# One root for two norms between two blocks, and the context normed during the last down projection

## The reference

```python
def rmsnorm(x, g):
    xf = x.astype(jnp.float32)
    y = xf * lax.rsqrt(jnp.mean(xf * xf, axis=-1, keepdims=True) + EPS)
    return (y * g.astype(jnp.float32)).astype(x.dtype)
...
        x = x + (jax.nn.silu(g) * u) @ w_down[i]
    return rmsnorm(x, final_g)
```

```python
def modulate(a, g, shift, scale):
    return rms_norm(a, g) * (1 + scale) + shift
...
        h_lat = modulate(x, norm_g[layer], sh_l, sc_l)
        h_ctx = modulate(ctx, norm_g[layer], sh_c, sc_c)
```

## Time and profile before

| | |
|---|---|
| median of 3 runs | 2828.7 us (2828.47 to 2835.98) |
| profiled execution | 2831.81 us, its span 2830.0 us |
| granted TensorE clock, mean | 0.963 |
| PE busy | 2604.9 us, 92% |
| PEld busy | 2114.6 us, 75% |
| DVE busy | 1117.6 us, 39% |
| ACT busy | 991.3 us, 35% |
| POOL busy | 975.6 us, 34% |

### The profile page before, as it was taken

How to read it: one execution, slowest core, us unless ns; L and a number is a source line. 1 busy time by engine, 2 the same in 40 slices (tenths; PEclk the granted TensorE clock), 3 DMA queues, 4 the chain that set the end, 5 groups by cost and what they waited for, 6 DMA issues and landing times.

```text
span 2830.0 us, 33844 instructions
## 1 busy us (share of the span) xinstructions
PE 2604.9 (92%) x13182; PEld 2114.6 (75%) x13182; DVE 1117.6 (39%) x2054; ACT 991.3 (35%) x1811; POOL 975.6 (34%) x515
## 2 busy tenths in 40 slices
PE   5999899999999989999869989999999998898888
PEld 4775688888676668888657878878877887786666
DVE  2136589520324559841151121430112242355564
ACT  3335344432434444442232232211222222344442
POOL 4322255754422135675432222322222222321121
PEclk9999899999999989999979999999999999899999
DMA  4111154222311125422211000111100021110000
GB/s 165 68 34 60 60 183 175 97 92 94 105 53 41 60 94 196 138 99 95 92 38 45 23 30 23 60 60 60 45 23 31 30 68 47 61 60 23 31 31 30
DMA packets 53869, 199.52 MB, mean 71 GB/s; under 512 B 5968, under 2 KB 5968, under 8 KB 52944
## 3 DMA queue, kind: packets, MB, share of 16 engines
q1 hardware_dynamic: 51696, 188.65, 19.5%
q10 hardware_dynamic: 2016, 8.71, 0.9%
HBM read 195.24 MB, written 2.10 MB: 70 GB/s over the span
## 4 chain that ended last, share of the span: by engine, by line
PE 85%; DVE 5%; ACT 3%; POOL 3%; issue 2%; DMA 1%; ACTq 0%; POOLq 0%; DVEq 0%
PE ps L507 54%; PE ps L527 12%; PE ps L557 7%; PE ps L832 5%; PE ps L704 3%; POOL wl L2182 1%; POOL norm_acc L2195 1%; PE ps L1026 1%; PE ps L719 1%; DVE norm_sq L1633 1%; ACT wh L1063 1%; PE ps L706 0%; POOL norm_sq L2277 0%; PE ps L839 0%; PE ps L1011 0%
## 5 line engine op out<-in xcount | busy, mean ns | idle before, releaser
L2182 POOL TENSOR_TENSOR wl<-wring,wh 128x1024 fp32r<-128x1024 f32 (+1 forms) x305 | 761.8, 2498 | 1418.5 <-ACT wh L1063 1408.1
L1063 ACT ACTIVATE wh<-wring 128x1024 fp32r<-128x1024 f32 (+1 forms) x305 | 317.0, 1042 | 771.4 <-PE ps L507 765.7
L507 PE MATMUL ps<-hh,wh 128*128 128x512 f32 x1224 | 481.7, 394 | 20.4 <-DVE hl L1645 16.0
L507 PE MATMUL ps<-hl,wh 128*128 128x512 f32 x1224 | 480.5, 393 | 0.0
L507 PE MATMUL ps<-hh,wl 128*128 128x512 f32 x1224 | 480.3, 392 | 0.0
L507 PEld LDWEIGHTS ps<-hh,wh 128*128 128x128 f32 x1224 | 232.1, 190 | 74.7 <-DVE hl L1645 15.7
L507 PEld LDWEIGHTS ps<-hh,wl 128*128 128x128 f32 x1224 | 231.6, 189 | 49.0
L507 PEld LDWEIGHTS ps<-hl,wh 128*128 128x128 f32 x1224 | 231.8, 189 | 47.3 <-issue 0.5
L557 PE MATMUL ps<-arena 128*128 128x64 f32 (+2 forms) x720 | 186.9, 396 | 14.4 <-ACT arena L1267 6.2
L1669 DVE CUSTOM_DVE_ANT_0 arena<-arena 128x1024 f32<-128x1024 f32 x96 | 185.8, 1935 | 9.0 <-DVE arena L1845 0.5
L557 PEld LDWEIGHTS ps<-arena 128*128 128x128 f32 x720 | 109.0, 197 | 85.3 <-issue 58.2
(11 more groups left out here) (263 smaller groups left out, 4941.4 us busy)
## 6 DMA issues: line engine op xcount, KB each, us to landing
wring<-wts SPq DMA_DIRECT2D x290, 512.0 KB, 3.5
arena<-wts SPq DMA_DIRECT2D x48, 512.0 KB, 4.3
wring<-wts SPq DMA_DIRECT2D x16, 384.0 KB, 2.9
xL<-xt SPq DMA_DIRECT2D x1, 2048.0 KB, 9.6
arena<-tab SPq DMA_DIRECT2D x1, 2048.0 KB, 16.8
arena<-cv ACTq DMA_DIRECT2D x2, 1024.0 KB, 5.5
arena<-tab ACTq DMA_DIRECT2D x1, 2048.0 KB, 9.0
out_t<-xL ACTq DMA_DIRECT2D x8, 256.0 KB, 2.0
```

Source lines behind the costliest of these rows:

```text
L507: mm = nc.tensor.matmul(o[0], a, b, start=start and k == first and j == 0, stop=stop and k == last and j == 2)
L1063: nc.scalar.activation(wh[:, sn % SPLIT_SLOTS, :kn * w], raw(u)[:, :kn * w], ACT.Copy).then_inc(act_done, tick("act", ("hi", u)))
L2182: G.tensor_tensor(wl[:, sn % SPLIT_SLOTS, :kn * w], raw(u)[:, :kn * w], wh[:, sn % SPLIT_SLOTS, :kn * w].bitcast(F32), ALU.subtract).then_inc(
```

## The change

- `mL` is no longer made from `fin`'s result. ScalarE squares each new `xL` tile twice during the down projection: once as it is (`fin`) and once scaled by `fgn[:, m]` (`mL`), the absolute final gain, made at the kernel's start by Square, Ln and Exp of eight columns. One root of the second sum, with `eps2` = EPS x EPS in place of EPS, scales `xL` straight to `hH` and `hLo`, with the gain `fgm` (final gain times modulation gain). `fin` gets its own scratch at `NF` and bank 6, and its root and scaling come after `mL`'s.
- The context is loaded into `xct`, over `hH`, after the last up projection, squared and added behind the split of `dn 0,1`, summed by TensorE after j = 0, its root made in j = 1, and its split pass done in j = 3, after the split of `dn 3,2` on ScalarE and before `xL` tile 6 on the vector engine. It is then loaded a second time, into `xC`.
- TensorE does the context's gate columns (now banks 4 and 5), `norm(("mL",0))`, the context's query columns, `norm(("fin",0))`, and then for each of the 8 tiles the latents' gate columns and both latent query tiles. `project_qk(0)` has only `("mqk",0,1)` left.
- The split of `("mqk",0,0)` moves between the last squares and additions.

The core of the diff:

```diff
-            norm(("fin", 0))
-            norm(("mC", 0))
-            norm(("mL", 0))
-            for m in range(KT):
-                pe.wait_ge(dve_done, at("dve", "hl", ("mC", 0), m))
+                    if l == DEPTH - 1 and j == 0:
+                        norm(("mC", 0))
...
-            def hm_ready(k):
+            (gate_unit,), query_units = views(("gate",)), views(("mqk", 0, 0))
+            gate_all, hc = slice(0, 100), (lambda k: hcH[:, k, :], lambda k: hcL[:, k, :])
+            for m in range(KT):
+                pe.wait_ge(dve_done, at("dve", "hl", ("mC", 0), m))
+            claim([4, 5], "dve", "glf")
+            product(ps[0:100, 4, 256:512], rows(gate_all, *hc), [gate_unit])
+            norm(("mL", 0))
+            for i in range(2):
+                claim([2 * i, 2 * i + 1], "act", "mqk", 0, i)
+            for u in query_units:
+                for i in range(2):
+                    product(ps[:, 2 * i, 256:512], rows(side(i), *hc), [u], start=u is query_units[0],
+                            stop=u is query_units[1])
+            norm(("fin", 0))
+            for k in range(KT):
                 pe.wait_ge(dve_done, at("dve", "hl", ("mL", 0), k))
-
-            claim([0, 1], "dve", "glf")
-            project(("gate",), both(0, 100, slice(0, 100), ("gate",)), hm_ready)
+                u, first, _, v = query_units[k // 4]
+                end = k == KT - 1
+                product(ps[0:100, 5, :], lat(gate_all), [(gate_unit[0], k, 1, [r[:, k:k + 1, :] for r in gate_unit[3]])],
+                        *([("gate",), ("used", gate_unit[0])] if end else []), start=k == 0, stop=end)
+                for i in range(2):
+                    product(ps[:, 2 * i + 1, :], lat(side(i)), [(u, k, 1, [r[:, k - first:k - first + 1, :] for r in v])],
+                            *([("mqk", 0, i)] if end else []), *([("used", u)] if i and k % 4 == 3 else []),
+                            start=k == 0, stop=end)
...
+            nc.scalar.activation(fgn[:, 0:8], col("fin", 0, 8), ACT.Square).then_inc(act_done, tick("act"))
+            act.wait_ge(act_done, now("act"))
+            nc.scalar.activation(fgn[:, 0:8], fgn[:, 0:8], ACT.Ln, bias=col("eps")).then_inc(act_done, tick("act"))
+            act.wait_ge(act_done, now("act"))
+            nc.scalar.activation(fgn[:, 0:8], fgn[:, 0:8], ACT.Exp, scale=0.5).then_inc(act_done, tick("act", ("fgn",)))
...
+                if last:
+                    act.wait_ge(pe_done, at("pe", "up", l, 2 * FT - 1))
+                    act.dma_start(xct.rearrange("p k t -> p (k t)"), ct).then_inc(ctx_loaded, 16)
+                    act.wait_ge(pool_done, at("pool", "gul", l, FT - 1))
+
+                def square_both(m):
+                    square(("mL", 0), m, ("xd", l), fgn[:, m:m + 1])
+                    square(("fin", 0), m, ("xd", l))
...
+                        if last and (j, c) == (0, 0):
+                            act.wait_ge(ctx_loaded, 16)
+                            for m in range(KT):
+                                square(("mC", 0), m)
+                        if last and (j, c) == (1, 0):
+                            root(("mC", 0))
+                        if last and (j, c) == (3, 1):
+                            high(("mC", 0), hcH, 1)
+                            act.wait_ge(pe_done, at("pe", "used", units_of[("dn", l, 3, 1)][-1]))
+                            act.dma_start(xC.rearrange("p k t -> p (k t)"), ct).then_inc(ctx_loaded, 16)
...
+            split(("mqk", 0, 0), first)
+            square_both(6)
+            square(("mL", 0), 7, ("xd", DEPTH - 1), fgn[:, 7:8])
+            split(("mqk", 0, 0), second)
+            square(("fin", 0), 7, ("xd", DEPTH - 1))
             root(("mL", 0))
             high(("mL", 0), hH, 0)
-            split(("mqk", 0, 0))
+            root(("fin", 0))
...
+                    if l == DEPTH - 1 and m == 6:
+                        dve.wait_ge(dve_done, now("dve"))
+                        V.tensor_tensor(fgn[:, 8:16], mscv[:, 0, 0, 0:8], col("fin", 0, 8), ALU.mult).then_inc(
+                            dve_done, tick("dve", ("fgm",)))
+                        dve.wait_ge(pe_done, at("pe", "used", units_of[("dn", l, 3, 0)][-1]))
+                        scaled_split(("mC", 0), lambda m: mscv[:, 0, 1, m:m + 1], hcH, hcL, 1)
...
+            scaled_split(("mL", 0), lambda m: fgn[:, 8 + m:9 + m], hH, hLo, 0)
             scaled(("fin", 0), lambda m: col("fin", m), xL)
-            scaled_split(("mC", 0), lambda m: mscv[:, 0, 1, m:m + 1], hcH, hcL, 1)
-            scaled_split(("mL", 0), lambda m: mscv[:, 0, 0, m:m + 1], hH, hLo, 0)
...
+                        if last and (j, c) == (0, 0):
+                            accumulate(("mC", 0))
...
+                    elif j < 3:
+                        for m in (2 * j, 2 * j + 1):
+                            accumulate(("mL", 0), m)
+                            accumulate(("fin", 0), m)
+            split(("mqk", 0, 0), slice(0, 1))
+            accumulate(("mL", 0), 6)
+            accumulate(("fin", 0), 6)
+            accumulate(("mL", 0), 7)
+            split(("mqk", 0, 0), slice(1, 2))
+            accumulate(("fin", 0), 7)
```

More of the change, by code:

```diff
@@ L132, in param_columns @@
     at, n = {}, 0
-    for name, width in [("eps", 1), ("ln1", 16), ("ln2", 16), ("fin", 8), ("ng", 16), ("qn", 4), ("kvn", 2),
+    for name, width in [("eps", 1), ("eps2", 1), ("ln1", 16), ("ln2", 16), ("fin", 8), ("ng", 16), ("qn", 4), ("kvn", 2),
                         ("dn", 2), ("fb", 2), ("conv", DEPTH * 4 * 2 * FT), ("lam", DEPTH * 256), ("adab", 48),
@@ L279, in program @@
         msc = place("msc", 32)[0]
+        fgn = place("fgn", 16)[0]
         arena, ar = place("arena", ARENA)
@@ L1309, in _ @@
                         load_exp_ln()
-                after = ("ln1", l + 1) if l + 1 < DEPTH else ("fin", 0)
+                last = l + 1 == DEPTH
+                if last:
[5 more added lines that the diff above has]
+                    square(("fin", 0), m, ("xd", l))
                 for j in range(4):
@@ L1314, in _ @@
                             split(("dn", l, j, c + 1) if c < 2 else ("dn", l, j + 1, 0))
[L1315 to L1330 removed]
+                        else:
+                            split(("gate",) if last else ("cq", l + 1))
+                        if last and (j, c) == (0, 0):
[8 more added lines that the diff above has]
+                            act.dma_start(xC.rearrange("p k t -> p (k t)"), ct).then_inc(ctx_loaded, 16)
+                    if not last:
+                        square(("ln1", l + 1), 2 * j, ("xd", l))
+                        square(("ln1", l + 1), 2 * j + 1, ("xd", l))
+                    elif j < 3:
+                        square_both(2 * j)
+                        square_both(2 * j + 1)
+            split(("mqk", 0, 0), first)
[3 more added lines that the diff above has]
+            square(("fin", 0), 7, ("xd", DEPTH - 1))
             root(("mL", 0))
             high(("mL", 0), hH, 0)
[L1333 removed]
+            root(("fin", 0))
             act.wait_ge(dve_done, at("dve", "glf"))
@@ L2263, in _ @@
                             split(("dn", l, j, c + 1) if c < 2 else ("dn", l, j + 1, 0))
-                        elif l + 1 < DEPTH:
-                            split(("cq", l + 1))
-                        else:
-                            split(("gate",))
-                    accumulate(after, 2 * j, 2 * j + 1)
-            accumulate(("mC", 0))
-            accumulate(("mL", 0))
-            split(("mqk", 0, 0))
+                        else:
+                            split(("gate",) if last else ("cq", l + 1))
+                        if last and (j, c) == (0, 0):
+                            accumulate(("mC", 0))
+                    if not last:
+                        accumulate(("ln1", l + 1), 2 * j, 2 * j + 1)
+                    elif j < 3:
+                        for m in (2 * j, 2 * j + 1):
[7 more added lines that the diff above has]
+            accumulate(("fin", 0), 7)
             def rows_norm(h):
@@ L2395, in layout @@
     put("eps", 0, np.full((P, 1), EPS, np.float32))
+    put("eps2", 0, np.full((P, 1), EPS * EPS, np.float32))
     put("idn", 0, np.eye(P, dtype=np.float32))
```

53 lines of the change are left out of this document (25 added, 28 removed).

## The result

The changed kernel takes 2803.68 us (median of 4 runs, 2797.8 to 2804.29) beside 2829.41 us for the kernel before on the same chip (2828.47 to 2835.98). The ratio is 0.9896, with a 95% interval of 0.9882 to 0.9910: 1.0% faster. The profiled execution took 2804.22 us with a span of 2802.2; the profiled one of before took 2831.8 with 2830.0. The forecast was 2800.6 us, with a range of 2795.5 to 2806.

A forecast was written before the change was run, and what follows sets the result against it. TensorE, busy 92% of the span, bounds the kernel; its standstills around the last down projection can be won. 28.75 us won less 0.7 at the start gives 28.05: 2828.7 to 2800.6 us, range 2795.5 to 2806.

The forecast's parts named there:

- Norm of `mC` between two chunks: Last down projection: the context's sum on TensorE between two chunks costs 0.5 us, between nothing and 1.12.
- No stall of the down projection: Context squares and doubled additions cost TensorE nothing there, with 3.0 us and 3.5 us of cover.
- rival B: Down projection stalls because squares or additions use up the cover; 2802 to 2806 us, chance 0.10.
- Pass of the context, 1.5 us added: Context's scaling pass during the down projection: 6.7 us plus 1.5 beside a GpSimd split, last high part at 1399.2.
- Rival A: Vector engine and GpSimd exclude each other only on scans, so added terms go: 2.7 us less, 2797.9; chance 0.12.
- C: Context not ready early; its pass and gate split slip behind the down projection: 2811 us, chance 0.04.
- Sum of `mL`, 1408.8: Behind the down projection: TensorE starts the norm of `mL` at 1408.8, after GpSimd's splits and additions.
- 1.25 us for the addition beside the pass: Latents' pass: GpSimd's last `fin` addition beside it adds 1.25 us by exclusion; term between 0 and 1.27.
- Eight steps at full clock: Latents' gate and query columns: 72 matmuls take 16.8 us without waiting, to 1433.1.
- rival D: TensorE stays at clock 0.50 through the eight steps after resting before the norm: +14.7 us, 2815; chance 0.04.
- What is late next: `fin` root and scaling, gate reads, soft-plus, then splits of `("mqk",0,1)`: TensorE idles 10.5 us, 1433.1 to 1443.6.
- The second half, 1443.6 to 1463.15: Query/key projection: second unit at 1446.6, 84 matmuls in 15.5 us, 1.05 for low clock; end at 1463.15.

The follow-up runs named there:

- e5: Changed kernel with two roots again: only `fin` squared in the down projection, `mL` squared from its scaled result; 2812.42 us, ratio 0.9944.
- e6: Changed kernel with splits and evacuations ahead of the soft-plus, plus four more moves, among them `fin` scaled behind the gate reads; 2796.98 us, ratio 0.9896.
- e1: Changed kernel with ScalarE's splits of `("mqk",0,1)` ahead of its wait for the gate reads; 2797.76 us, ratio 0.9886.
- e7: Changed kernel with ScalarE's splits of `("mqk",0,1)` and evacuations of the first two query banks ahead of its wait for the gate reads; 2792.42 us, ratio 0.9872.
- after: The changed kernel itself, first profiled execution, against the kernel before; median 2803.68 us, ratio 0.9896.
- e2: Changed kernel with TensorE's reordered loop undone: latents' gate columns alone in the loop, then the whole query/key projection; 2803.72 us, ratio 0.99.
- e4: Changed kernel with the context's squares, sum, root and pass behind the down projection again; 2822.21 us, ratio 0.9972.

## Why the prediction was right, point by point

Times of after are 6.24 us later than mine (1410.24 for 1404.0), by what lies ahead of the stage.

- *Norm of `mC` between two chunks, 0.5 us.* The record stands at 1316.86, two matmuls, 0.59 us, and keeps TensorE from the next for 0.43. Right.
- *No stall of the down projection.* TensorE has no wait from 1300 to 1404. The cover of 3.0 and 3.5 us was enough; rival B is out, for this case.
- *Pass of the context, 1.5 us added.* GpSimd's split at 1397.20 takes 1.85, and the low part beside it 1.77 where it takes 0.48 alone: 1.3. The last high part ends at 1404.97; mine gives 1405.4. Rivals A and C are out. The lines, from the timelines of GpSimd and the vector engine:

```profile
1397.20 1.85 POOL L2234 TENSOR_TENSOR wl<-wring,wh 128x768 fp32r<-128x768 f32 x1 [3.77 <-ACT wh L1086]
...
1397.55 1.77 DVE L1687 SCALAR_TENSOR_TENSOR hc_l<-arena,mod,hc_h 128x256 fp32r<-128x256 f32 x1 [6.08 <-ACT hc_h L1114]
```

- *Sum of `mL`, 1408.8.* It starts at 1414.67, mine with the shift 1415.0, after a wait of 1.6 us (I said about 2). The pass starts 2.55 us behind it, at 1417.22, as read from the earlier trace rows.
- *1.25 us for the addition beside the pass.* The exclusion holds for additions too: the first two scalings take 2.45 us instead of 1.41, which is 1.04. `e5` and `e6` show it at full size. By the Trainium skill (GPSIMD Engine Reference, 8. Key points) GpSimd contends with vector instructions that have two SBUF inputs; the traces agree, with 9.44 us for 5.39 and 9.31 us for 2.4.
- *Eight steps at full clock (rival D).* From 1413.5 to 1438.7 the granted clock is 1.00. D is out. TensorE stops at 1438.7; mine gives 1439.3.
- *What is late next.* The chain is the one named: root of `fin`, scaling (5.39), memsets, gate reads, which end at 1440.12 + 1.02 = 1441.14 (mine 1442.1), soft-plus, split of 3.90 us, ready 7.55 us behind the gate reads (mine 7.59). The wait is 10.1 us (mine 10.5), the largest of the stage. `e1` and `e7` show that this order cost the time: 3.5 us for the splits and 3.8 more for the evacuations.
- *The second half, 1443.6 to 1463.15, is the step that was off.* It took 18.40 us, I had 19.55. My 19.55 is 3.0 us up to the second unit, with the first twelve matmuls hidden in it, then 84 matmuls in 15.5, and 1.05 for low clock until 5.1 us after the restart. The low clock lasted only 3.3 us here. From the windows:

```profile
1448.82:1452.12 3.30, 3.30 (x15) 3.29 (x16) 3.27 (x2) 0.00 (x0) 3.16 (x2) 0.50 0.48 159
```

  Most of it fell on the first twelve matmuls, which filled the time up to the second unit, so that little of it cost time: the 84 matmuls from 1451.52 took 15.70 us where I had 16.55. That is 0.85 of the 1.15 us. Why the clock rose earlier than in the earlier trace rows isn't shown. The other 0.3 us are the second unit, with which TensorE began 2.70 us behind the first and not 3.0. I let GpSimd wait for the scan before it, as in the earlier trace rows; here the scan waited:

```profile
1449.26 3.21 DVE L1934 TENSOR_TENSOR_SCAN arena<-arena 4x512 f32<-4x512 f32 x1
1452.50 2.98 DVE L1940 TENSOR_TENSOR arena<-arena 36x768 f32<-36x768 f32 x1
```

  The same shapes take 1.27 and 0.95 us later in this trace. GpSimd's three splits run one behind the other from 1444.79 to 1454.68 (3.89, 2.57 and 3.14 us), and the vector engine's delay costs nothing there.
- *Rival A's price.* The terms that it removes are 1.5, 1.25 and 0.5 us in my sum, 3.25 together; I had written 1.25 for the first and 2.7 in all. With A out, nothing hangs on it.
- *The sum.* The stage is 57.0 us, mine was 1463.15 - 1404.0 = 59.15: 2.2 us better, 1.0 of it at the gate reads and 1.2 in the second half. The start costs 0.8 us (mine 0.7). The mechanism held, and its sizes to about 1 us. That the spans differ by 27.8 us, so near my 28.05, is luck: the stage won 2.2 us more than forecast, 3.1 us behind it are no work of the change, and 6.7 us were lost ahead of it where I had 0.7 and 0.5. The median of 2803.68 lies 3.1 above the forecast although the stage did better; the same kernel's median on another chip, 2799.31, lies 1.3 below it. What separates them is of the size of the clock stretch at 230 us, 6.3 us, which was in neither my sum nor my range's terms; whether it is that stretch isn't shown.

## What to carry to other kernels

When a stage is a chain over three engines, write down for each moved step what it leaves uncovered: here the norms' waits went, and 10 us of the gain stood behind a soft-plus that earlier had 16.9 us of matmuls over it; putting the splits and the evacuations of finished banks before the engine's wait gave back 7.3 us. Before moving an elementwise pass, look at what GpSimd does at that time: eight scalings off one engine's path made a 2.4 us split on another's take 9.3. Judge a change of a few microseconds by the length of its own stage between two landmarks, not by the whole time.

Up to rounding the single root is exact, and the wording "absolute final gain" of the change hides why: `fgn` is the root of g x g + EPS, since Ln has EPS as its bias. The mean of (x fgn)^2 is then the mean of (x g)^2 plus EPS times the mean of x^2, and with EPS x EPS added that is just what the second norm divides by when the first is put into it.

## What the runs showed of the hardware

- In these traces GpSimd and the vector engine hold each other up where both read two SBUF operands, and which of them waits varies. Beside a single instruction the one that waits loses about the rest of the other (a low part of 0.48 becomes 1.77 beside a split that keeps its 1.85; a scan of 1.27 becomes 3.21 beside a split of 2.57). Beside a dense row it is much more: 2.4 becomes 9.31 beside eight scalings of 5.38 in all and an instruction of 0.94, although the split's record starts 0.86 us ahead of them (`e6`). In that case the scalings lost nothing, GpSimd everything; in `e5`, with short additions, both lost (5.39 becomes 9.44, and 9.7 for seven additions with their gaps becomes 11.21).
- The granted clock has stretches of about 14 us at its lower level that are there in one execution and not in the next of the same kernel, with TensorE as busy as ever (13.07 of 14.00 us at 0.54, 12.89 at 1.00). This one was in three of thirteen traces (`after`, `e2`, `e4`) and is worth 6.3 us of 2800, nearly what the two reorderings of ScalarE in `e7` gave back (7.3). A second, at 900 to 1000 us, was in every trace of one family of kernels (five of thirteen). What brings either about wasn't found.
